# Feed-forward block of a four-stage encoder kernel: 2x2 blocks by seven products for two of three token groups, with weight sums on GpSimd and a ring of weight units

## The reference, cut to what matters

```python
def residual_update(x, h_m, attn, w_out, g_post_mix, g_pre_ffn, w_ffn_in, w_ffn_out, g_post_ffn):
    x = x + rmsnorm(jnp.concatenate([h_m, attn], axis=-1) @ w_out, g_post_mix)
    h = rmsnorm(x, g_pre_ffn)
    gate, up = jnp.split(h @ w_ffn_in, 2, axis=-1)
    return x + rmsnorm((jax.nn.silu(gate) * up) @ w_ffn_out, g_post_ffn)
```

## Time and profile before

| | before |
|---|---|
| median of three executions | 3014.78 us |
| the profiled execution, its span | 3010.2 us |
| TensorE busy | 2956.3 us, 98% |
| VectorE busy | 1272.8 us, 42% |
| ScalarE busy | 589.5 us, 20% |
| GpSimd busy | 998.7 us, 33% |
| moved by DMA | 137.16 MB, mean 46 GB/s |

### The profile page before, as it was taken

The page is one execution under the profiler, slowest core; times in us unless marked ns, Lnnn a source line. Parts: engine busy times, 40 slices in busy tenths (PEclk is TensorE's granted clock), DMA queues, the critical chain, the costliest instruction groups (busy, mean ns, idle before and its releaser), DMA issues.

```text
span 3010.2 us, 42170 instructions
## 1 busy us (share of the span) xinstructions
PE 2956.3 (98%) x17729; PEld 2755.1 (92%) x17729; DVE 1272.8 (42%) x1565; ACT 589.5 (20%) x1034; POOL 998.7 (33%) x468
## 2 busy tenths in 40 slices
PE   8999999999999999999999999999999999999998
PEld 8999967788999999999989998676989999999997
DVE  7333345546433223233583334465472232333326
ACT  4222234523000000000241213345130000000003
POOL 2222233233343434333322222422524343333441
PEclk9999989999999999999999999999999999999999
DMA  5222210021111111111122112100301111111111
GB/s 167 40 39 37 34 34 1 1 93 43 42 49 49 42 49 42 48 49 42 33 86 53 30 30 37 31 1 8 114 22 50 49 42 49 49 42 42 42 53 61
DMA packets 200046, 137.16 MB, mean 46 GB/s; under 512 B 38888, under 2 KB 191096, under 8 KB 199424
## 3 DMA queue, kind: packets, MB, share of 16 engines
q1 hardware_dynamic: 187248, 111.01, 13.8%
q10 hardware_dynamic: 12688, 24.59, 2.2%
HBM read 119.64 MB, written 15.94 MB: 45 GB/s over the span
## 4 chain that ended last, share of the span: by engine, by line
PE 74%; issue 12%; DVE 5%; POOLq 5%; ACT 2%; DVEq 1%; POOL 1%; ACTq 0%; DMA 0%
PE acc L623 17%; PE acc L626 17%; PE acc L627 17%; PE acc L1149 5%; PE acc L1152 5%; PE acc L1153 5%; DVE residual L1741 1%; POOLq L547 1%; POOLq L550 1%; PE acc L793 1%; DVE branch L1739 1%; PE acc L775 1%; DVE x_square L1755 1%; DVEq L1740 1%; PE acc L591 1%
## 5 line engine op out<-in xcount | busy, mean ns | idle before, releaser
L623 PE MATMUL acc<-act_hi,slab_hi 128*128 128x352 f32 x2640 | 859.9, 326 | 6.6 <-ACT residual L1393 5.2
L627 PE MATMUL acc<-act_lo,slab_hi 128*128 128x352 f32 x2640 | 846.4, 321 | 0.0
L626 PE MATMUL acc<-act_hi,slab_lo 128*128 128x352 f32 x2640 | 846.1, 321 | 0.0
L451 POOL TENSOR_TENSOR slab_hi<-slab_raw,ones 128x1024 fp32r<-128x1024 f32 x141 | 272.0, 1929 | 993.7 <-PE acc L623 561.5
L623 PEld LDWEIGHTS acc<-act_hi,slab_hi 128*128 128x128 f32 x2640 | 495.2, 188 | 13.3 <-issue 8.6
L626 PEld LDWEIGHTS acc<-act_hi,slab_lo 128*128 128x128 f32 x2640 | 496.7, 188 | 0.0
L627 PEld LDWEIGHTS acc<-act_lo,slab_hi 128*128 128x128 f32 x2640 | 495.0, 187 | 0.0
L2164 DVE TENSOR_TENSOR branch<-acc,branch 128x1056 f32<-128x1056 f32 x160 | 201.1, 1257 | 389.7 <-PE acc L1153 389.7
L453 POOL TENSOR_TENSOR slab_lo<-slab_raw,slab_hi 128x1024 fp32r<-128x1024 f32 x141 | 358.5, 2542 | 21.0 <-issue 0.6
L2154 DVE TENSOR_TENSOR work<-acc,work 128x1056 f32<-128x1056 f32 x44 | 55.2, 1255 | 568.9 <-PE acc L627 568.9
L451 POOL TENSOR_TENSOR small_hi<-slab_raw,ones 128x1024 fp32r<-128x1024 f32 x50 | 95.8, 1917 | 594.4 <-PE acc L623 508.0
(11 more groups left out here) (401 smaller groups left out, 4918.1 us busy)
## 6 DMA issues: line engine op xcount, KB each, us to landing
slab_raw<-in_w_ffn_in SPq DMA_DIRECT2D x88, 512.0 KB, 3.7
slab_raw<-in_w_ffn_out SPq DMA_DIRECT2D x44, 512.0 KB, 3.2
slab_raw<-in_w_in SPq DMA_DIRECT2D x40, 512.0 KB, 3.9
x_spill<-residual ACTq DMA_DIRECT2D x2, 4224.0 KB, 12.6
residual<-x_spill ACTq DMA_DIRECT2D x2, 4224.0 KB, 14.0
slab_raw<-in_w_out SPq DMA_DIRECT2D x16, 512.0 KB, 3.8
out_y_prompt<-out_rows SPq DMA_DIRECT2D x8, 512.0 KB, 3.9
branch<-in_x_prompt ACTq DMA_DIRECT2D x2, 1024.0 KB, 6.5
```

The costliest lines, as they stand in the source:

```text
L451: pool.tensor_tensor(hi, raw, ONES[:, 0:1].broadcast_to([P, SLAB]), ALU.mult)
L623: mm = pe.matmul(out, wh, HH[:, x], start=k == 0, stop=False)
L626: pe.matmul(out, wl, HH[:, x], start=False, stop=False)
L627: mm = pe.matmul(out, wh, HL[:, x], start=False, stop=k == KT - 1)
```

## The change

In each layer the first pair is done as before (gate and up of tiles 0 and 1), and the gates of tiles 2 and 3 too. For all that follows, the output product of the last pair excepted, a product of a pair is taken as blocks: the weights of two tiles as 2x2 (two tiles by two halves of the inner dimension: A11, A12, A21, A22), and the activations of token groups 0 and 1 by the same halves. The four blocks of the result are made by seven block products in place of eight, with four sums of weight blocks (S1 = A21 + A22, S2 = S1 - A11, S3 = A11 - A21, S4 = A12 - S2) and four sums of activation blocks (T1 to T4). Group 2 is done without them, with A11 to A22 as they are. The steps of such a product are called a round. In a long round (gate or up of a pair) there are 11 steps `wide` of 4 x 3 = 12 matmuls, 132 in all. The output product takes two half rounds, each 66 matmuls in `short` steps. Per layer there is one long round (up) and then BODIES = 9 times a gate round, two half rounds and an up round.

**TensorE.** The result chains lie in single banks: 0 (a), 2 (x), 4 (y), 6 and 7 (c); bank 2 is filled three times in a round. Each time VectorE or ScalarE must have taken the one before (`x_out`, `a_out`, `y_out`, `c_out`).

**GpSimd** no longer makes hi. In `weave` it forms S1 to S4 in place in four quarters Q11 to Q22 of `slab_raw` (each 128x512) and makes lo of each of the eight units (A21, A11, S3, A12, S2, A22, S1, S4). In half rounds units are 128x256. **ScalarE** makes hi of each unit by a copy (`hi_unit`), once the ring has room. The ring has 12 slots of 256 columns, so six units of 512. **SyncE** loads a quarter when GpSimd has freed it (`q_free`).

**VectorE** adds the chains (`chains`), in an up round multiplies by the gates, makes the sums of the inner activation for the next half rounds, and makes lo of nine pieces, 352 wide. In half rounds it adds 704 wide pieces to `branch` or to `first_products` (EP), which is added to three quarters of `branch` at the end. The sums of `h` are made in X: so X is written to memory (`f_spill`) behind the norm and read back behind the last up round (4224 KB each way). The table of angles (`trig`) is loaded anew, since its place is used too. Semaphores are shared between uses that don't meet (`in_turned_then_a_done`, `row_spread_then_x_done`, `gain_turned_then_y_done` and the like), with other counts and the same waits.

```diff
-FFN_STEPS = ((1, 14), (2, 1), (0, 15), (1, 15), (2, 2), (0, 16))
-FFN_LAST = ((1, 34), (2, 21), (0, 35), (1, 35), (2, 22))
...
+FFN_PLAIN = ((1, 14), (2, 1), (0, 14), (1, 15), (2, 2), (0, 15), (1, 16), (2, 3))
+A21, A11, S3, A12, S2, A22, S1, S4 = range(8)
...
+LONG_FREED = (0, 1, 2, 4, 3, 7, 5, 6)
...
+GATE_SLOTS = tuple((4 + 2 * _k) % 12 for _k in range(8))
...
+        QUAD = [RAW[:, i * BANK:(i + 1) * BANK] for i in range(4)]
...
+            if slot >= 8:
+                at = 2 * T + (slot - 8) * 256
+                return RH[:, at + c0:at + c1], RL[:, at + c0:at + c1]
+            return SH[:, slot * 256 + c0:slot * 256 + c1], SL[:, slot * 256 + c0:slot * 256 + c1]
...
+                        sp.wait_ge(q_free, 4 * (l * QUADS_ALL + sets - 1) + (3, 4, 1, 2)[q])
...
+                    sp.dma_start(dst, source).then_inc(q_landed[q], 16)
...
+                def lo_unit(made, k, slot, q, c0, c1):
+                    hi, lo = ring(slot, 0, c1 - c0)
+                    pool.wait_ge(unit_hi, UNIT_HI + l * MADE_ALL + made + k + 1)
+                    pool.tensor_tensor(lo, QUAD[q][:, c0:c1], hi, ALU.subtract).then_inc(unit_ready, 1)
+                def weave(made, sets, slots, c0=0, c1=BANK, frees=True):
...
+                    lo_unit(made, A21, slots[A21], Q21, c0, c1)
+                    pool.drain()
+                    pool.wait_ge(q_landed[Q11], landed)
+                    pool.tensor_tensor(q21, q11, q21, ALU.subtract).then_inc(unit_sum, 1)
+                    lo_unit(made, A11, slots[A11], Q11, c0, c1)
+                    lo_unit(made, S3, slots[S3], Q21, c0, c1)
+                    pool.drain()
+                    pool.wait_ge(q_landed[Q22], landed)
+                    pool.tensor_tensor(q21, q22, q21, ALU.subtract).then_inc(unit_sum, 1)
+                    lo_unit(made, A12, slots[A12], Q12, c0, c1)
+                    lo_unit(made, S2, slots[S2], Q21, c0, c1)
+                    pool.drain()
+                    pool.tensor_tensor(q11, q21, q11, ALU.add).then_inc(unit_sum, 1)
+                    pool.tensor_tensor(q12, q12, q21, ALU.subtract).then_inc(unit_sum, 1)
+                    if frees:
+                        pool.drain().then_inc(q_free, 1)
+                    lo_unit(made, A22, slots[A22], Q22, c0, c1)
+                    if frees:
+                        pool.drain().then_inc(q_free, 1)
+                    lo_unit(made, S1, slots[S1], Q11, c0, c1)
...
+                weave(0, 0, UP_SLOTS)
+                with pool.Fori(0, BODIES) as b:
+                    made = 8 + MADE * b
+                    weave(made, 1 + 3 * b, GATE_SLOTS)
+                    weave(made + 8, 2 + 3 * b, OUT_SLOTS[0], 0, 256, False)
+                    weave(made + 16, 2 + 3 * b, OUT_SLOTS[1], 256, 512)
+                    weave(made + 24, 3 + 3 * b, UP_SLOTS)
...
+                def wide(b, slot, moving, first, last, gives=None):
+                    for k in range(4):
+                        wh, wl = ring(slot, k * P, (k + 1) * P)
+                        xh, xl = moving(k)
+                        mm = pe.matmul(bank(b, TG), wh, xh, start=first and k == 0, stop=False, skip_group_check=True)
+                        if k == 0 and gives is not None:
+                            mm.then_inc(gives, 1)
+                        pe.matmul(bank(b, TG), wl, xh, start=False, stop=False, skip_group_check=True)
+                        mm = pe.matmul(bank(b, TG), wh, xl, start=False, stop=last and k == 3, skip_group_check=True)
+                    return mm
...
+                    made_by(A21)
...
+                    wide(7, slots[A21], h13, True, False, unit_used)
...
+                    wide(0, slots[A11], h11, True, True, unit_used).then_inc(a_done, 1)
+                    wide(6, slots[A11], h13, True, False)
...
+                        pe.wait_ge(y_out, Y_OUT + 2 * (l * ROUNDS + r))
+                    wide(4, slots[S3], h_t3, True, True, unit_used).then_inc(y_done, 1)
...
+                        pe.wait_ge(x_out, X_OUT + 3 * (l * ROUNDS + r))
+                    wide(2, slots[S2], h_t2, True, True, unit_used).then_inc(x_done, 1)
+                    pe.wait_ge(a_out, A_OUT + 2 * (l * ROUNDS + r) + 1)
+                    wide(0, slots[A12], h21, False, True, unit_used).then_inc(a_done, 1)
...
+                    pe.wait_ge(x_out, X_OUT + 3 * (l * ROUNDS + r) + 1)
+                    wide(2, slots[S1], h_t1, False, True, unit_used).then_inc(x_done, 1)
+                    wide(7, slots[A22], h23, False, True, unit_used).then_inc(c_done, 1)
+                    made_by(S4)
+                    pe.wait_ge(x_out, X_OUT + 3 * (l * ROUNDS + r) + 2)
+                    wide(2, slots[S4], h22, False, True).then_inc(x_done, 1)
...
+                    pe.wait_ge(y_out, Y_OUT + 2 * (l * ROUNDS + r) + 1)
+                    wide(4, slots[A22], h_t4, False, True, unit_used).then_inc(y_done, 1)
...
+                long_round(0, 0, UP_SLOTS, True)
+                with pe.Fori(0, BODIES) as b:
+                    made = 8 + MADE * b
+                    long_round(1 + 4 * b, made, GATE_SLOTS)
+                    pe.wait_ge(g_ready, G_READY + l * (4 + BODIES) + 4 + b + 1)
+                    half_round(2 + 4 * b, made + 8, OUT_SLOTS[0])
+                    half_round(3 + 4 * b, made + 16, OUT_SLOTS[1])
+                    long_round(4 + 4 * b, made + 24, UP_SLOTS)
...
+                    act.activation(ring(slot, 0, c1 - c0)[0], QUAD[q][:, c0:c1], ACT.Copy).then_inc(unit_hi, 1)
...
+                def gate_round(b):
...
+                    gates(b, S1)
+                    act.wait_ge(g_part, l * PARTS_ALL + 4 + 6 * b + 4)
+                    first_product(1 + 4 * b, part(W2, 0, 1))
+                    gates(b, S4)
+                    outs(b, 0, A21)
+                    outs(b, 0, A11)
...
+                    act.activation(part(W2, 0, 2), bank(6, TG), ACT.Silu).then_inc(c_out, 1)
+                    outs(b, 0, S3)
...
+                def chains(r, c12, c21, c22, between, behind):
...
+                    dve.wait_ge(x_done, X_DONE + 3 * r + 1)
+                    dve.tensor_tensor(c21, bank(2, TG), c12, ALU.add).then_inc(x_out, 1)
+                    between()
+                    dve.wait_ge(x_done, X_DONE + 3 * r + 2)
+                    dve.tensor_tensor(c22, bank(2, TG), c12, ALU.add).then_inc(x_out, 1)
...
+                def gate_round(b):
...
+                    chains(r, c12, c21, c22, lambda: None, lambda: None)
...
+                def up_round(i, last=False):
...
+                        dve.tensor_tensor(f(1, 1), f(1, 1), unit_of(W2, 1, 1), ALU.mult).then_inc(g_part, 1)
...
+                    dve.tensor_tensor(g12, f(0, 1), g12, ALU.mult)
+                    dve.drain()
+                    dve.tensor_tensor(f(0, 1), g12, f(0, 0), ALU.subtract).then_inc(g_part, 1)
...
+                    dve.tensor_tensor(GTF[0][:, :], f(1, 1), f(0, 1), ALU.subtract).then_inc(g_part, 1)
+                    dve.tensor_tensor(GTF[1][:, :], f(1, 1), g12, ALU.subtract).then_inc(g_part, 1)
+                    dve.wait_ge(y_done, Y_DONE + 2 * r + 2)
+                    dve.tensor_tensor(f(1, 0), bank(4, TG), f(1, 0), ALU.add).then_inc(y_out, 1)
+                    dve.drain()
+                    if not isinstance(i, int) or i:
+                        gates(3)
+                    dve.tensor_tensor(f(1, 0), f(1, 0), unit_of(W2, 1, 0), ALU.mult).then_inc(g_part, 1)
+                    dve.drain()
+                    dve.tensor_tensor(GTF[2][:, :], f(1, 0), GTF[0][:, :], ALU.subtract).then_inc(g_part, 1)
+                    lo(his + 1, 0, 0)
...
+                    g_lo_part(his + 9, GTL[0][:, :], GTF[0][:, :], GTH[0][:, :])
+                    g_lo_part(his + 9, GTL[2][:, :], GTF[2][:, :], GTH[2][:, :])
+                    dve.drain().then_inc(g_ready, 1)
```

More of the change, by code:

```diff
@@ L1219, in _ @@
                 sum_group(2, 4, KT)
[L1220 removed]
+                for slot in (1, 2):
                     pe.drain().then_inc(slab_free[slot], 1)
@@ new lines, in _ @@
+                t_hi_part(2, TXH[0][:, :], TXF[0][:, :])
+                t_hi_part(1, quarter(HH, 0, 1), by(EP[:, :], 4))
+                t_hi_part(4, TXH[2][:, :], TXF[2][:, :])
+                for unit in range(6):
+                    first_up(unit)
+                up_round(0, first_up, lambda unit: gates(0, unit))
+                with act.Fori(0, BODIES - 1) as b:
+                    body(b)
+                body(BODIES - 1, True)
+                act.wait_ge(y_done, Y_DONE + 2 * (l + 1) * ROUNDS)
```

597 lines of the change are left out of this document (480 added, 117 removed).

## The result

The changed kernel takes **3044.79 us** in the median of 4 runs (3039.75 to 3057.72); beside it the kernel before took 3016.11 (3003.78 to 3024.35). The ratio on record is 1.0112, 95% interval [1.0075, 1.0148] (the quotient of the two medians is 1.0095): slower by about 1%, and above the range of 2922 to 3035 us. 672 matmuls are gone and the kernel is slower.

What follows compares the result with a forecast made beforehand. TensorE, busy 98% of the span, was taken as the bound: 3010.2 - 106.6 (matmuls) + 45 (stall) + 7 (second stall) + 9 (edges) = 2964.6 us, with 4.6 for the median about 2970 us; range 2922 to 3035 us.

Steps and rivals of the forecast that it cites:

- second stall: Second half rounds: the fifth unit's slots free 0.95 us ahead, hi and lo need 1.35; 0.4 us late, 7 us in all.
- stall at line 2631: Gate round, eighth step: VectorE, held up by GpSimd, empties bank 2 2.5 us too late, 18 times, 45 us.
- edges: Start and end of each layer's loop: late lo parts, sums of h and reading X back, together 9 us.
- The step that failed: TensorE's matmul price: every matmul keeps its shape, so each still costs 0.1586 us.
- matmuls slower with 0.1586 us exceeded without waits: Sign in the loop's stretches that the forecast is wrong: each matmul costs more than 0.1586 us though TensorE does not wait.
- the point from which nothing is won: Gate-round stall at which the saved matmuls are used up: (106.6 - 16) / 18 = 5.0 us.
- Matmuls removed: TensorE: rounds of 132 matmuls replace 144, so 672 matmuls or 106.6 us are gone.
- GpSimd's work: GpSimd per loop body: 47.3 us of instructions, 59.5 of 62.8 us with gaps and delays; busy some 85% of the loop.
- Taking turns: VectorE instructions with two SBUF inputs alternate with GpSimd's; line 2654 averages 1 to 1.6 us; accumulator reads are not held.
- no stall: Rival: GpSimd is ahead or its sums miss VectorE's work, so no gate-round stall; 2922 us, chance 0.15.
- GpSimd as bound: Rival: GpSimd's 256-column instructions cost 1.04 us, its body 67.7 us, so it bounds the loop; 3005 us, chance 0.19.
- VectorE falls behind: Rival: in the gate round GpSimd is three units late, making the stall 8.2 us; 3071 us, chance 0.14.

Runs made afterwards that it cites:

- the last kernel: Changed kernel with five lo parts after line 2631, S3 taken before S2 in half rounds, three lo parts before the last up round's last add: 2926.93 us.
- the kernel with 13 filler matmuls: Changed kernel plus 13 unused identity matmuls of 128 columns on TensorE before its wait for line 2631 in each gate round: 3013.10 us.
- that with four parts: Changed kernel with four of VectorE's nine lo parts left ahead of line 2631 in gate rounds and five moved behind it: 2953.15 us.

## Why the prediction was wrong

The loops' sum in the runs' own steps, each step one experiment: 1329.1 (matmuls alone) + 14.7 (left in the last kernel) + 6.8 (tail) + 15.7 (second stall) + 59.3 (stall at line 2631: the kernel with 13 filler matmuls less that with four parts, 1425.6 - 1366.3) + 35.1 (half clock: the changed kernel less that with the filler, 1460.7 - 1425.6) = 1460.7 us. The prediction had 45 + 7 + 9 = 61 us on top of 1329, the runs 131.6. The missing 70.6 us: clock 35.1, stall 14.3, second stall 8.7, edges 12.5. Without the clock's 35.1 the time would have been about 3010 us, inside the range.

**The step that failed** is "Every matmul keeps its shape, 352 columns behind a load of 128x128, so I leave 0.1586 us." The price came from a stretch without a gap, and I then forecast 18 gaps of 2.5 us into it and kept the price. In the earlier trace rows one slice of the clock stands lower than the others, and I did not ask what TensorE had done ahead of it. So the forecast had the clock behind a gap at 0 us, without a reason, and the runs showed 35.1. None of the rivals had it either; "matmuls slower with 0.1586 us exceeded without waits" stood only among the signs of being wrong. The prediction put the point from which nothing is won at 5.0 us a body, with 16 us of other costs; stall and clock are (59.3 + 35.1) / 18 = 5.2 us. With the other costs as they were, 15.7 + 21.5 = 37.2 us, the point is (106.6 - 37.2) / 18 = 3.9 us, so its 5.0 comes near by luck.

**Matmuls removed**: right, 672, 106.6 us.

**GpSimd's work**: the prices right, the load a little less than forecast. By line and shape (busy, mean ns, idle before):

```profile
L692 POOL TENSOR_TENSOR slab_lo<-slab_raw,slab_hi 128x512 fp32r<-128x512 f32 x232 | 311.2, 1341 | 117.7 <-ACT slab_hi L1942 82.3 <-issue 30.2 <-ACT small_hi L1942 4.6
...
L692 POOL TENSOR_TENSOR small_lo<-slab_raw,small_hi 128x256 fp32r<-128x256 f32 x144 | 110.7, 769 | 140.7 <-ACT small_hi L1942 122.3 <-issue 18.4
```

256 columns take 0.74 us where nothing disturbs them (priced 0.70), 512 take 1.29 (1.27). GpSimd is busy for 494.18 of 728.30 us, 68%, and for 49.2 us in a body, 71% of its 69.3 (the sign named was 85% of the loop; 47.3 + 5 us a body were forecast), and idle before both kinds mostly because ScalarE's hi isn't there yet. It is never the bound: that rival (0.19) is out.

**Taking turns**: right. VectorE by line:

```profile
L2728 DVE TENSOR_TENSOR branch<-acc,branch 128x704 f32<-128x704 f32 x288 | 256.9, 892 | 88.1 <-PE acc L1394 74.0
L2654 DVE TENSOR_TENSOR small_lo<-small_lo_f,small_hi 128x352 fp32r<-128x352 f32 x120 | 163.7, 1417 | 0.0
```

1417 ns in the mean for what takes 0.52 alone ("1 to 1.6 us"; the 54 lo parts of `g_t_f`, made by the same line, took 788), and 892 for an add of 704 columns out of the accumulator ("about 0.87"), which isn't held.

**The stall at line 2631**: the mechanism and the count of 18 right, the size 3.3 us for 2.5. VectorE, then GpSimd, ahead of the stall above:

```profile
1069.33 0.52 DVE L2640 TENSOR_TENSOR small_lo_f<-acc,small_lo_f 128x352 f32<-128x352 f32 x1 [1.27 <-PE acc L1330]
...
1071.74 0.52 DVE L2701 TENSOR_TENSOR g_t_f<-small_lo_f,work 128x352 f32<-128x352 f32 x1
1072.17 0.52 DVE L2703 TENSOR_TENSOR small_lo_f<-acc,small_lo_f 128x352 f32<-128x352 f32 x1
1072.85 0.94 DVE L2707 TENSOR_TENSOR small_lo_f<-small_lo_f,work 128x352 f32<-128x352 f32 x1 [0.16 <-issue]
1073.88 1.45 DVE L2709 TENSOR_TENSOR g_t_f<-small_lo_f,g_t_f 128x352 f32<-128x352 f32 x1
1075.25 7.80 DVE L2654 TENSOR_TENSOR small_lo<-small_lo_f,small_hi 128x352 fp32r<-128x352 f32 x5
...
1087.11 0.53 DVE L2631 TENSOR_TENSOR work<-acc,work 128x352 f32<-128x352 f32 x1 [0.70 <-issue]
```

```profile
1073.37 1.58 POOL L692 TENSOR_TENSOR slab_lo<-slab_raw,slab_hi 128x512 fp32r<-128x512 f32 x1
...
1081.38 1.29 POOL L692 TENSOR_TENSOR slab_lo<-slab_raw,slab_hi 128x512 fp32r<-128x512 f32 x1 [0.26 <-ACT small_hi L1942]
1082.92 0.73 POOL L692 TENSOR_TENSOR small_lo<-slab_raw,small_hi 128x256 fp32r<-128x256 f32 x1 [0.25 <-issue]
...
1084.60 1.00 POOL L692 TENSOR_TENSOR small_lo<-slab_raw,small_hi 128x256 fp32r<-128x256 f32 x1
```

The gate round's first matmul starts at 1071.04, so bank 2 is due at 1071.04 + 13.3 = 1084.4. From the start of line 2703 to that of line 2631 it took 14.94 us; the prediction had 15.1 - 0.2 = 14.9. (Two more instructions of 256 columns came in, at 1083.89 and 1084.60; the first of 512, from 1072.11, lay mostly beside an add that isn't held.) But it started line 2703 1.13 us behind t = 0, not 0.2: the sums of lines 2696 to 2701, which follow the chain of the step before, were still in work. That is the 0.8 to 0.9 us that were missed, 18 times. (The upper bound of 9.5 us doesn't follow from its terms: 15 instructions of 0.53 us that each wait 1.13 more come to above 11 us. The sum didn't use it.)

**The second stall**: 15.7 us for 7. TensorE, ScalarE and GpSimd in one:

```profile
1107.41 0.32 PE L1394 MATMUL acc<-small_lo,slab_hi 128*128 128x352 f32 x1
1108.40 0.42 PE L1390 MATMUL acc<-small_hi,slab_hi 128*128 128x352 f32 x1 [0.68 <-POOL small_lo L692]
```

```profile
1107.04 0.72 ACT L1942 ACTIVATE small_hi<-slab_raw 128x256 fp32r<-128x256 f32 x2 [5.27 <-PE acc L1390]
```

```profile
1107.53 0.72 POOL L692 TENSOR_TENSOR small_lo<-slab_raw,small_hi 128x256 fp32r<-128x256 f32 x1 [3.54 <-ACT small_hi L1942]
```

From ScalarE's start to TensorE's it takes 1.36 us, for which 1.35 was worked out. But the slot is free only 0.53 us before the unit is due (1107.57), not 0.95: the step's first matmul starts at 1106.60 and must end, and the message must arrive, before ScalarE begins. So 0.83 us is lost each time, not 0.4.

**The edges**: 21.5 us for 9, of which the tail's wait is 6.8. The tail's 6.8 have the 3.1 of two low stretches in them. The other 14.7 are still in the last kernel and were not taken apart.

**The rivals**: no stall (0.15) is out, GpSimd as bound (0.19) too. "VectorE falls behind" gave 0.14 to stalls near 8 us; they are 3.3. The result has the sign of that rival without its mechanism.
